# Seven products instead of eight for the value tiles, too: a float32 transformer stack in split precision on one core

## The reference

```python
def rmsnorm_2(x, g):
    xf = x.astype(jnp.float32)
    y = xf * lax.rsqrt(jnp.mean(xf * xf, axis=-1, keepdims=True) + EPS)
    return (y * g.astype(jnp.float32)).astype(x.dtype)

def swiglu(h, wg, wu, wd):
    return (jax.nn.silu(h @ wg) * (h @ wu)) @ wd

    for i in range(DEPTH_2):
        x = x + 0.5 * swiglu(rmsnorm_2(x, ffn_norm1[i]), ffn1_wg[i], ffn1_wu[i], ffn1_wd[i])
        ...
        x = x + 0.5 * swiglu(rmsnorm_2(x, ffn_norm2[i]), ffn2_wg[i], ffn2_wu[i], ffn2_wd[i])
```

## Time and profile before

| | us |
|---|---|
| median of 3 runs | 2646.99 (2646.88 to 2649.75) |
| the profiled execution, its own time | 2647.2 |
| its span, first to last instruction | 2645.9 |
| TensorE busy | 2616.8 (99%) |
| VectorE busy | 1556.7 (59%) |
| ScalarE busy | 1076.6 (41%) |
| GpSimd busy | 561.6 (21%) |

### The profile page before, as it was taken

The page is one execution under the profiler, slowest core; times in us unless marked ns, Lnnn a source line. Parts: engine busy times, 40 slices in busy tenths (PEclk is TensorE's granted clock), DMA queues, the critical chain, the costliest instruction groups (busy, mean ns, idle before and its releaser), DMA issues.

```text
span 2645.9 us, 33136 instructions
## 1 busy us (share of the span) xinstructions
PE 2616.8 (99%) x13424; PEld 2228.0 (84%) x13424; DVE 1556.7 (59%) x2398; ACT 1076.6 (41%) x1782; POOL 561.6 (21%) x556
## 2 busy tenths in 40 slices
PE   9999999999999999999999999999999989999999
PEld 8888888888887788779988888888988888888888
DVE  7637547565757445356777565564646677564653
ACT  4334334342454222236754233442423586443332
POOL 0000010000021000015541323121322587323230
PEclk9999999999999999999999999999999999999999
DMA  5332325523233444454422232323333101332322
GB/s 162 114 101 87 97 80 175 171 80 111 73 103 96 108 104 92 104 103 114 111 86 94 91 113 89 103 80 96 104 103 95 56 29 33 96 105 71 127 80 80
DMA packets 276400, 259.05 MB, mean 98 GB/s; under 512 B 40324, under 2 KB 266647, under 8 KB 276247
## 3 DMA queue, kind: packets, MB, share of 16 engines
q1 hardware_dynamic: 276231, 256.93, 32.4%
q10 hardware_dynamic: 16, 0.00, 0.0%
HBM read 242.23 MB, written 14.68 MB: 97 GB/s over the span
## 4 chain that ended last, share of the span: by engine, by line
PE 89%; DVE 4%; ACT 3%; issue 2%; POOL 2%; POOLq 0%; ACTq 0%; DVEq 0%
PE bank L1478 26%; PE bank L1480 26%; PE bank L1479 26%; PE bank L1578 3%; PE bank L1579 3%; PE bank L1580 3%; PE bank L1666 1%; DVE Wl L2290 1%; DVE Pl L2313 0%; PE bank L1730 0%; ACT Wh L1879 0%; POOL Wl L2903 0%; ACT Z L2214 0%; POOL TMP L2944 0%; DVE bank L2404 0%
## 5 line engine op out<-in xcount | busy, mean ns | idle before, releaser
L1478 PE MATMUL bank<-Hh,Wl 128*128 128x512 f32 x1752 | 688.6, 393 | 1.2 <-DVE Hl L2356 0.8
L1480 PE MATMUL bank<-Hh,Wh 128*128 128x512 f32 x1752 | 682.2, 389 | 0.0
L1479 PE MATMUL bank<-Hl,Wh 128*128 128x512 f32 x1752 | 682.1, 389 | 0.0
L2290 DVE TENSOR_TENSOR Wl<-RAW,Wh 128x1024 fp32r<-128x1024 f32 (+1 forms) x324 | 389.9, 1247 | 148.7 <-ACT Wh L1879 148.1
L1879 ACT ACTIVATE Wh<-RAW 128x1024 fp32r<-128x1024 f32 (+2 forms) x358 | 345.2, 1015 | 274.5 <-PE bank L1480 204.9
L1478 PE MATMUL bank<-Ph,Wl 128*128 128x512 f32 x1152 | 451.9, 392 | 0.8 <-DVE Wl L2290 0.4
L1480 PE MATMUL bank<-Ph,Wh 128*128 128x512 f32 x1152 | 448.6, 389 | 0.0
L1479 PE MATMUL bank<-Pl,Wh 128*128 128x512 f32 x1152 | 448.2, 389 | 0.0
L1478 PEld LDWEIGHTS bank<-Hh,Wl 128*128 128x128 f32 x1752 | 329.1, 188 | 71.7 <-issue 1.7
L1480 PEld LDWEIGHTS bank<-Hh,Wh 128*128 128x128 f32 x1752 | 328.9, 188 | 69.0
L1479 PEld LDWEIGHTS bank<-Hl,Wh 128*128 128x128 f32 x1752 | 329.1, 188 | 68.0 <-issue 1.7
(11 more groups left out here) (387 smaller groups left out, 3937.5 us busy)
## 6 DMA issues: line engine op xcount, KB each, us to landing
RAW<-in_ffn_wg SPq DMA_DIRECT2D x44, 1024.0 KB, 5.3
RAW<-in_ffn_wu SPq DMA_DIRECT2D x44, 1024.0 KB, 5.3
RAW<-in_ffn_wd SPq DMA_DIRECT2D x32, 1024.0 KB, 5.3
RAW<-in_w_up SPq DMA_DIRECT2D x22, 1024.0 KB, 5.1
RAW<-in_w_in SPq DMA_DIRECT2D x20, 1024.0 KB, 5.2
RAW<-in_ffn_wd SPq DMA_DIRECT2D x16, 768.0 KB, 4.4
bias_scratch<-M SPq DMA_DIRECT2D x16, 512.0 KB, 7.9
RAW<-in_w_down SPq DMA_DIRECT2D x8, 1024.0 KB, 5.2
```

The source lines that it names most:

```text
L1478: mm(o, ll, rh, start=start, stop=False)
L1479: mm(o, lh, rl, start=False, stop=False)
L1480: return mm(o, lh, rh, start=False, stop=stop)
L2290: tt(wflat(Wl, o + x, o + y), RAW[:, n % 2, x:y], f(wflat(Wh, o + x, o + y)), ALU.subtract).then_inc(*w_lo.up(*([("w_lo", n)] if i else [])))
```

## The change

`BOTH` names 18 pairs: all of the second and third third of `s1` and `s2`, and of the second third of `s3`. In these the value tile is computed by seven products as well. `pair_both` writes such a pair by two calls of `seven`, which has four hooks at which other steps are put: the pieces of the next tile, the silus, the multiplication of gate and value. The two operands of that multiplication (`glu_f`) now both come from SBUF. Four more slots for results are taken from `Z` while these tiles run. Pieces 1 and 2 of a value tile go to the region that its whole tile had. For the first changed tile of a part (the gate tile of the fourth pair) piece 2 is filled earlier and piece 3 later than before.

```diff
+BOTH = {"s1": ((1, 0), (1, 1), (1, 2), (1, 3), (2, 0), (2, 1), (2, 2)), "s2": ((1, 0), (1, 1), (1, 2), (1, 3), (2, 0), (2, 1), (2, 2)),
+        "s3": ((1, 0), (1, 1), (1, 2), (1, 3))}
...
 def is_seven(tile):
     name, key = tile[0:2]
-    return name[:-1] in SEVEN and name[-1] == "a" and key >= (0, FIRST_SEVEN)
+    tag, x = name[:-1], name[-1]
+    return tag in SEVEN and (x == "a" and key >= (0, FIRST_SEVEN) or x == "b" and key in BOTH[tag])
...
             do("cp", n, 1, t)
             tail()
+            if (h, j) == (0, FIRST_SEVEN):
+                feed(n, 3)
             do("c11", n, t)
...
+        def seven(n, t, first, second, third, fourth):
+            prod(n, 1)
+            prod(n, 2)
+            for c in range(2):
+                tmps.take(t[c])
+            do("cp", n, 1, t)
+            first()
+            do("c11", n, t)
+            prod(n, 6)
+            do("cp", n, 2, t)
+            second()
+            prod(n, 5, 0, 2)
+            prod(n, 7)
+            do("cp", n, 3, t)
+            prod(n, 5, 2, 4)
+            do("c22", n, t)
+            third()
+            prod(n, 4)
+            do("c21", n, t, now["norm"])
+            do("rm", n, 1, t, now["norm"])
+            fourth()
+            prod(n, 3)
+            do("c12", n, t)
+            do("rm", n, 0, t, now["norm"])
+
+        def pair_both(h, j, last_pair):
+            n = next_tile(tag + "a", (h, j), 0)
+            t, u = ([(name, tag, h, j, c) for c in range(2)] for name in ("t_a", "t_b"))
+            feed(n + 1, "sums")
+            seven(n, t, tail, lambda: feed(n + 1, 0, 4), lambda: feed(n + 1, 1), lambda: feed(n + 1, 2))
+            feed(n + 1, 3)
+            nb = next_tile(tag + "b", (h, j), 0)
+
+            def finish_both(m):
+                do("glu_f", nb, m, t[m], u[m])
+                pair_p(2 * j + m, "tmp", t[m], ("glu", t[m]))
+
+            def silus():
+                for m in (1, 0):
+                    do("silu_f", n, m, t)
+                if not last_pair:
+                    feed(n + 2, "sums")
+
+            def prepare():
+                if last_pair:
+                    plain(n + 2)
+                else:
+                    feed(n + 2, 0, 4)
+
+            def prepare_more():
+                if last_pair:
+                    plain(n + 3)
+                else:
+                    feed(n + 2, 1)
+
+            seven(nb, u, silus, prepare, prepare_more, lambda: finish_both(1))
+            feed(n + 2, 2, 3)
+            tails.append(lambda: finish_both(0))
...
             if leads:
-                feed(na + 2, 0, 4)
+                feed(na + 2, 0, 4, 2)
             combine(COMBOS[2 * j])
             dense(bb[1:2], nb, 8, "H", kw=1)
             do("used", nb)
-            feed(na + 2, 2, 3)
...
+            elif kind == "glu_f":
+                nb, m, t, u = s
+                dve.wait_ge(*at(("silu", t)))
+                dve.wait_ge(*at(("rm", nb, m)))
+                dve.wait_ge(*at(("c21", nb)))
+                tt(tmp(t), tmp(t), tmp(u), ALU.mult).then_inc(*dve_out.up(("glu", t), free=u))
```

More of the change, by code:

```diff
@@ L223, in places @@
             elif is_seven(tiles[n]):
-                pieces = [(2048 * ends + 1024 * side, 1024), (2048 * mid, 1024), (2048 * mid + 1024, 1024)]
+                region = mid if x == "a" else other
+                pieces = [(2048 * ends + 1024 * side, 1024), (2048 * region, 1024), (2048 * region + 1024, 1024)]
                 side = 1 - side
@@ L598, in ffn_seven @@
             if last:
+                tmps.slots, tmps.holder, tmps.i = tmps.slots[:3], tmps.holder[:3], -1
+                do("mark", "z_done")
                 todo[:] = [lambda i=i: x_turn(i // 4, i % 4) for i in range(8)]
@@ L602, in ffn_seven @@
                     assert not combos
-                    pair_seven(h, j, j == n // 2 - 1)
+                    if (h, j) == (0, FIRST_SEVEN):
+                        tmps.join(Ring((4, 5, 6, 7), home, before))
+                    (pair_both if (h, j) in BOTH[tag] else pair_seven)(h, j, j == n // 2 - 1)
                 else:
@@ L606, in ffn_seven @@
             tail()
+            if h == 2 and not last:
+                tmps.slots, tmps.holder, tmps.i = tmps.slots[:3], tmps.holder[:3], -1
             if h == 2:
@@ L1274, in bank @@
         return BANK[home[name]][:, :]
-    def tmp(name):
-        return TMP[:, home[name], 16:528]
     def vacated(name):
@@ L1389, in wflat, with tmp @@
         return W[:, :, :].rearrange("p a b -> p (a b)")[:, x:y]
+    def tmp(name):
+        i = home[name]
+        return TMP[:, i, 16:528] if i < 4 else Z[:, 512 * (i - 4):512 * (i - 3)]
     def weights(n, vi):
@@ L1918, in act_program @@
                 v = tmp(t[m]) if k == 2 else vacant(t[m])
+                if home[t[m]] > 3:
+                    act.wait_ge(*at(("hc_lo", tiles[n][0][:-1], 2)))
                 z = 0 if k == 1 else 256
@@ L2066, in act_program @@
                 if "s3" in SEVEN:
+                    all_gone("z_done")
                     for r in (2, 3):
```

## The result

The changed kernel took 2700.45 us (median of 4 runs, 2696.49 to 2704.20), the one before 2648.27 (4 runs, 2646.88 to 2649.75). The ratio is 1.0197, with a 95% interval of 1.0184 to 1.0210: slower by 52 us. Forecast were 2690 and, for the likeliest case alone, 2675 to 2705. The profiled execution took 2700.0 us, its span is 2698.8, its mean granted clock 0.993 (before: 2647.2, 2645.9 and 0.999).

What follows compares the result with a forecast made beforehand. TensorE bound the kernel before; after, VectorE and GpSimd excluding each other at SBUF would stall it. First pairs -4.3, 13 others +46.2, ends +1.5: +43.4 on 2647.2, said as 2690 us; 8-in-10 range 2660 to 2712.

Steps and rivals of the forecast that it cites:

- the likeliest case: Whole kernel: VectorE and GpSimd take turns at SBUF and stall TensorE; 2690 us, own range 2675 to 2705, chance 0.63.
- first pairs of a third: Five first changed pairs run undisturbed in 20.2 us, each -0.85, together -4.3 us.
- stall before product 6, then 7: Gate tile after a changed pair: TensorE waits for late copies, losing 1.4 us, then 2.6 us.
- gate tile, value tile in mid-third: Mid-third pair: gate tile 14.4 us with stalls, value tile 10.25, together 24.6 us.
- 18 tiles by seven instead of eight: Each converted value tile saves about 0.80 us of TensorE; 18 tiles save 14.3 us.
- stalls of 13 gate tiles, with what else lengthens such a pair: The 13 changed pairs that aren't first in a third take 3.55 us more each, +46.2 us net.
- ends of thirds: First d tile after a third waits for the late last split: 0.75 us, twice, +1.5 us.
- reorder at the first changed tile: New order of pieces at the first changed tile: counted at nothing, between -1.4 and +1 us a part.
- clock: Rival: TensorE's clock falls to 1.2 GHz behind the stalls of 13 pairs, +38 us atop, 2728; chance 0.03.
- hidden: Rival: preparation stays hidden behind TensorE, which keeps its 14.3 us; 2633, or 2642 with late second copies; chance 0.09.
- 22.5 us of holds: VectorE and GpSimd hold their shared SBUF port 22.5 us per changed pair; rival at this floor: 2662 us, chance 0.15.
- backlog in both tiles: Rival: the pile of late work also delays the value tile's copies; pair 26.5 us, 2714 in all; chance 0.10.

Runs made afterwards that it cites:

- The run with memsets: Changed kernel with GpSimd's sums, fourth sum and row factors replaced by constant fills of about like length, that computation left out: 2638.26 us, ratio 0.9964.
- the mended order: Against the kernel with 10 of 18 pairs changed: both splits behind the next gate tile's second copy, second product between pieces 2 and 3; 2648.83 us.
- the version with every other pair: Changed kernel with only 10 of the 18 pairs given the seven-product value tile, the last of each third among them: 2657.07 us, ratio 1.0035.
- the run without row factors: Changed kernel with GpSimd's row factors replaced by memsets of like length, its four sums kept real: 2675.12 us, ratio 1.0100.

## Why the prediction was right

The terms of the sum, against the two profiled executions (2700.0 - 2647.2 = 52.8 us):

| term | forecast | measured |
|---|---|---|
| first pairs of a third | 20.2 us | 10.08 + 10.16 = 20.24 |
| stall before product 6, then 7 | 1.4, 2.6 | 0.76 to 1.85 (mean 1.2), 2.40 each |
| gate tile, value tile in mid-third | 14.4, 10.25 | 13.9 to 14.2 at full clock, 15.1 to 16.3 with a fall; 10.16 |
| 18 tiles by seven instead of eight | 18 x -0.85 = -15.3 | -13.1 (10.18 in the mean for 10.90) |
| stalls of 13 gate tiles, with what else lengthens such a pair | 13 x (3.55 + 0.85) = 57.2 | 46.9, and 13 x 0.37 = 4.8 behind them: 51.7 |
| ends of thirds | +1.5 (twice 0.75) | +2.4 (waits of 0.96 and 0.88, and slower starts behind them) |
| reorder at the first changed tile | 0 | -0.3 in the profile, 2647.71 alone against 2647.34 |
| clock | 0 in the forecast | 8 x 1.5 = +12 |

51.7 - 13.1 + 2.4 - 0.3 = +40.7 without the clock, against +43.4 forecast, and +52.7 with it. The attention part adds 0.6, and the part ahead of the first changed tile takes 0.4 off.

**The mechanism** was right as laid out: both copies stand behind splits in ScalarE's queue, the splits wait for products of gate and value (3.88 us, twice), and these for row factors and pieces that VectorE and GpSimd draw out in turns. The run with memsets shows that this costs all of the loss: 2638 without it, which is the rival "hidden" (2633 to 2642) at its own price.

**The mis-sized term** is the clock. It was given a chance of 0.03 and a price of +38, for a fall behind both stalls in all 13 tiles; it fell in 8 of them, once in each, behind the second stall. The 12 us of the table overstate it, since each fall shortened the next stall. With the clock kept up by added matmuls the 13 gate tiles came to 189.9 - 13 x 10.15 = 58.0 us over undisturbed ones, where the forecast had 57.2: the stalls were sized right, and the falls took the sum from 58.0 to 63.6. So the clock cost 5.6 us net in the profiled execution, and 4.1 by the medians (2700.45 against 2696.31). The rest of the 9.4 us by which 2690.6 was short is mainly the smaller gain of the value tiles (2.2) and the ends (0.9).

The argument against a fall, a wait of 2.6 us in the kernel before, was read wrongly. The matmuls right behind that very wait ran at the lower level:

```profile
2117.18:2120.30 3.12, 3.12 (x12) 2.83 (x13) 1.42 (x3) 2.74 (x9) 1.05 (x3) 0.50 0.53 204
```

A mean clock of 0.999 over the whole span hides it. In the changed kernel each of the 8 falls begins between 0.3 us before the end of the stall of 2.40 us and 1.5 us behind it. The runs of the changed kernel spread with the clock, 2696.49 at a mean of 0.996 and 2704.20 at 0.992. The Trainium skill ("TensorE: Matmul & The Clock Gate", Part 1) says that the lower state follows idling and that where a fall lands is not tied to the kernel; with 8 of 13 like tiles hit, the trace agrees.

**A reason that fell.** The prediction called 22.5 us of holds the floor of a pair, "near the floor that the port sets", and priced a rival by it. A pair in mid-third did take 24.0 us and more at full clock, but holds of 20.6, 19.4 and 19.0 a pair gave 2708, 2704 and 2675 us, and 13.2 still a stall in every gate tile. What fits all these runs is the length of one row of steps, last combination, row factor, product, split, copy, against the 5.0 us (42 x 0.12) from a tile's start until product 7 is due. The lock lengthens its steps, by about 0.5 us in the mean and by 0.9 to 1.1 in the tile shown, and every instruction queued ahead of them on VectorE or ScalarE adds its own. Whether the floor exists at 22.5 stays open: the mended order was tried with every other pair changed, not with all 18.

**Value tiles** stayed clean, as forecast: the case "backlog in both tiles" didn't come. It did come in the version with the row factors on VectorE (value tiles with a stall of about 1.0 us), by another cause.

## What to carry to other kernels

Where VectorE and GpSimd both read two operands from SBUF, lay out the one row of dependent steps that ends at TensorE's next bank, with the turns of the two engines in it, before converting more work to that form; the busy shares (61% and 27% here) didn't show it. Put an operation that waits for a late product behind everything in its in-order queue that TensorE needs sooner, and make all inputs of such a group before its first member: the two together gave 8 us in the version with every other pair. Moving the splits with the inputs still made one by one only shifted the stall, in the version with all pairs; which of the two differences made it fail wasn't tested. Price a stall of TensorE with what the clock may take behind it, less what the stall after that gets shorter. And look at the granted clock of the stretch behind a wait before using that wait as proof that the clock holds: a mean over the run doesn't tell.

## What the runs showed of the hardware

- GpSimd's memsets don't lengthen VectorE's operations with two SBUF operands: 1222 ns in the mean, 1453 with sums and row factors.
- Moving an elementwise job from GpSimd to VectorE shortens it (row factor of 512 columns, means of 1.73 and 1.78 us on GpSimd and of 1.01 and 1.15 on VectorE) and still cost time here, 2700 to 2708 us.
- Stalls of the same lengths, about 1.27 and 2.40 us, were followed by a clock at its lower level in four tiles and not in a fifth. 24 added matmuls a tile kept it at 1.00 in every gate tile. In the run without row factors (stalls of 0.7 to 1.6 and of 1.3 us, 13 tiles) and in that with every other pair (1.3 and 1.3 us, 5 tiles) it stayed at 1.00 without them.
- A fall of the clock costs its tile 1.5 us and the kernel less, about half, since the engines that were late catch up meanwhile.
